# Fusing three stages of a transformer block: mixer output, row norm and the FFN up product in one program block

## The chip, the cores and the metric

The kernel runs on one core of a Trainium2 chip. The metric is device time in microseconds, the median of several runs; smaller is better. All arithmetic is float32. The large products are made of three passes in a rounded form of float32 (float32r): each factor is split into a high part (a copy rounded to float32r) and a low part (what is left), and high times high, high times low and low times high are summed.

## The reference, cut to what matters

```python
def rwkv_output(y, r, k, v, g_lo, lp):            # y: sum of a forward and a backward scan
    mu = mean(y, head); var = mean((y - mu)**2, head)
    yn = (y - mu) * rsqrt(var + GN_EPS) * ln_g + ln_b
    bonus = sum(r * k * r_k, head) * v
    return (yn + bonus) * (sigmoid(g_lo) @ g_up)

out_x = concat([y_conv, y_rwkv], -1) @ w_out      # both halves 512 wide, w_out 1024 x 1024
x = x + g1 * out_x
hx = rms_norm(x, norm2_g) * (1 + sc2) + sh2
gate, val = split(hx @ ffn_w_up, 2)               # 2816 wide each
gate = dwconv_grid(gate, 3 x 3) + b               # on a 16 x 64 grid of tokens
x = x + g2 * ((silu(gate) * val) @ ffn_w_down)
```

There are 1024 tokens and 1024 features. A second block (attention and others) follows and is not touched.

## The kernel before, in words

Activations lie feature-major: 128 partitions are 128 features, the free axis holds 1024 tokens, and KD = 8 feature tiles make the width. A PSUM bank holds 512 float32 per partition, so the tokens are worked in two halves, g = 0 and 1. Each stage is a program block of its own. Every engine has its own list of instructions, written out by hand; engines wait on semaphores. At the end of a stage all engines meet in a barrier, then the next stage starts. DMAs of these stages are issued by SyncE (SP) alone, in program order.

**scan** has 20 steps (4 over a context, 16 over the tokens, 64 tokens each), and each step does both directions (x = 0 forward, x = 1 backward). In one step TensorE's order is `token_major(s+1)`, `chain_g(s)`, `triangles`, `chain_z(s)`, `triangles`, `chain_s(s)`, `level_y`, `chain_y(s)`, `last_u`. VectorE does `triangles` (L1373), `chain_s` (L1378, L1380) and then a part of `blocks` (an inverse of small matrices, L1396 and others; its last part is in step 13). ScalarE copies TensorE's results out of PSUM, among them `chain_y`, which copies the step's output to a small buffer `yo`. SP stores it to DRAM (`store_y`, L1071, `ys`). GpSimd only makes a transposed copy five times (L1481). The results of the short convolution (`mixd`, tiles 0 to 3) and the bonus (`mixd`, tiles 4 to 7) were stored to DRAM by an earlier stage.

**mixer_out** loads forward and backward `ys` (L1511), adds them on GpSimd (L1648), and for each of four feature tiles j (PAIRS = 4) makes the group norm: head mean by a product with a matrix of ones (L1533), `centred` (L1672), square (L1600), head variance (L1544), Sqrt (L1607), reciprocal (L1678) and product (L1680), gain (L1612), bonus (L1686), gate product (L1551) and gating (L1690), high part (L1617) and low part (L1653, L1706). Then the output product: 8 output tiles n, each 2 token halves, 8 feature tiles k and 3 passes, 384 matmuls (tile 0 at L1577, the others at L105), each result added to x1 by VectorE (L1716). Weights are split as they come (L1594, L1642).

**norm_x1** works in four groups of 256 tokens: squares (L1741), sums by a product with ones (L1774), Sqrt (L1747), reciprocal (L1781), product (L1787), shift (L1760), high (L1764) and low (L1800, L1812). SP loads the first FFN weights beside it (L1806).

**ffn_up** runs a loop over 22 tiles. Each has a gate tile (s = 0) and a value tile (s = 1), each in two token halves of 24 matmuls (L105), 96 in all. ScalarE copies the gate to a grid (L1881), VectorE does nine taps (L1930, L1928), ScalarE takes Silu (L1887), VectorE multiplies with the value (L1936). The next tile's weights are split by ScalarE (L1875) and GpSimd (L1904); the high part of s = 1 is split only after the Silu.

## Time and profile before

| what | value |
|---|---|
| time, median of 3 runs | 2567.75 us (2562.33 to 2571.12) |
| the profiled execution's own time | 2575.16 us |
| its span, first to last instruction | 2573.4 us |
| busy: TensorE, VectorE, ScalarE, GpSimd | 2255.2, 1483.8, 847.4, 567.9 us |
| mean granted TensorE clock | 0.942 |

The stages follow one another in time, so the time of a stretch between two barriers can be read off the timeline. The busy shares over the whole span are averages over stages with different limits. A matmul's listed duration is longer than its share of TensorE's time, because matmuls overlap: the rate is read from starts.

### The profile page before, as it was taken

To read this page: it belongs to the slowest core of one execution; us is meant where nothing else is said; L and a number is where in the kernel's file an instruction comes from. 1 tells how busy PE (TensorE), PEld (TensorE's weight loads), DVE (VectorE), ACT (ScalarE), POOL (GpSimd) and SP (SyncE) were. 2 spreads that over 40 slices of the span, in tenths; PEclk is the share of its full clock that TensorE was granted. 3 is DMA by queue.
4 is the path that set the end of the run, shared out by engine and by line. 5 is a ranking of instruction groups with operands and counts; after the bars stand their busy time and mean duration, and the time that the engine had idled before them with its cause. 6 is when DMAs were issued, how large, how long until landed. Compare 5 with 4: busy or idle time off the path is not lost. (4 is left out here: it accounts for less than half of the span.)

```text
span 2573.4 us, 44358 instructions
## 1 busy us (share of the span) xinstructions
PE 2255.2 (88%) x18308; PEld 1777.2 (69%) x18308; DVE 1483.8 (58%) x1859; ACT 847.4 (33%) x1291; POOL 567.9 (22%) x256
## 2 busy tenths in 40 slices
PE   6879999558989779599999996889999999999898
PEld 1747777458988557478887885767767766676566
DVE  5886776777663352566666664026364656735653
ACT  4333444123323321433333322125243433423321
POOL 0334443100000141322222221323422111111111
PEclk8989999879999889799999998999999999999899
DMA  6644234666565510021221114342321111011412
GB/s 255 227 149 135 101 111 145 179 165 158 131 152 130 229 42 33 17 73 73 73 73 63 64 69 151 118 141 79 126 83 55 52 58 58 34 50 42 180 66 74
DMA packets 261015, 271.14 MB, mean 105 GB/s; under 512 B 173544, under 2 KB 204904, under 8 KB 255600
## 3 DMA queue, kind: packets, MB, share of 16 engines
q1 hardware_dynamic: 256240, 251.94, 30.6%
q10 hardware_dynamic: 4608, 16.78, 1.8%
q8 instruction: 128, 2.10, 0.4%
q14 instruction: 39, 0.32, 0.0%
HBM read 200.48 MB, written 68.19 MB: 104 GB/s over the span
## 5 line engine op out<-in xcount | busy, mean ns | idle before, releaser
L105 PE MATMUL b_ps<-h_hi,b_wpool 128*128 128x512 f32 (+1 forms) x976 | 301.9, 387 | 19.6 <-issue 7.5
L105 PE MATMUL e_ps<-h_hi,e_w_hi 128*128 128x512 f32 x704 | 276.0, 392 | 32.6 <-POOL e_w_lo L1904 32.2
L1928 DVE SCALAR_TENSOR_TENSOR e_acc<-e_grid,vec,e_acc 128x1024 f32<-128x1024 f32 x176 | 265.6, 1509 | 42.7 <-DVE e_acc L1928 37.4
L105 PE MATMUL e_ps<-h_lo,e_w_hi 128*128 128x512 f32 x704 | 274.8, 390 | 0.0
L105 PE MATMUL e_ps<-h_hi,e_w_lo 128*128 128x512 f32 x704 | 274.6, 390 | 0.0
L2451 PE MATMUL g_ps<-g_h_hi,w 128*128 128x512 f32 x784 | 260.0, 403 | 4.9 <-ACT g_q L2644 4.9
L105 PEld LDWEIGHTS b_ps<-h_hi,b_wpool 128*128 128x128 f32 x976 | 183.4, 193 | 68.3 <-issue 20.3
L1904 POOL TENSOR_TENSOR e_w_lo<-raw_up,e_w_hi 128x1024 fp32r<-128x1024 f32 x44 | 115.4, 2624 | 372.6 <-ACT e_w_hi L1875 372.6
L2764 POOL TENSOR_TENSOR w<-raw_down,w 128x1024 fp32r<-128x1024 f32 x38 | 93.8, 2469 | 462.9 <-ACT w L2622 462.9
L105 PE MATMUL b_ps<-h_lo,b_wpool 128*128 128x512 f32 (+1 forms) x488 | 185.3, 380 | 0.0
L105 PEld LDWEIGHTS e_ps<-h_hi,e_w_hi 128*128 128x128 f32 x704 | 132.6, 188 | 66.4 <-issue 39.2
L2005 PE MATMUL g_pb<-g_z_hi,g_down_hi 128*128 128x512 f32 x330 | 137.3, 416 | 46.5 <-POOL g_down_lo L2147 27.3
L2451 PEld LDWEIGHTS g_ps<-g_h_hi,w 128*128 128x128 f32 x784 | 148.3, 189 | 40.5 <-ACT g_q L2644 5.6
L2451 PE MATMUL g_ps<-g_h_lo,w 128*128 128x512 f32 x392 | 155.5, 397 | 0.0
L105 PEld LDWEIGHTS e_ps<-h_hi,e_w_lo 128*128 128x128 f32 x704 | 132.6, 188 | 27.7
L105 PEld LDWEIGHTS e_ps<-h_lo,e_w_hi 128*128 128x128 f32 x704 | 132.6, 188 | 27.0
L2147 POOL TENSOR_TENSOR g_down_lo<-raw_down,g_down_hi 128x1408 fp32r<-128x1408 f32 x29 | 93.9, 3242 | 198.0 <-ACT g_down_hi L2063 198.0
L2005 PE MATMUL g_pb<-g_z_hi,g_down_lo 128*128 128x512 f32 x330 | 135.0, 409 | 0.0
L2005 PE MATMUL g_pb<-g_z_lo,g_down_hi 128*128 128x512 f32 x330 | 134.2, 407 | 0.0
L2005 PEld LDWEIGHTS g_pb<-g_z_hi,g_down_hi 128*128 128x128 f32 x330 | 65.0, 197 | 65.3 <-POOL g_down_lo L2147 29.4
L105 PEld LDWEIGHTS b_ps<-h_lo,b_wpool 128*128 128x128 f32 x488 | 94.4, 194 | 17.2 <-issue 1.8
L714 POOL TENSOR_TENSOR b_wpool<-raw_in,b_wpool 128x1024 fp32r<-128x1024 f32 x26 | 66.9, 2573 | 170.4 <-ACT b_wpool L512 170.4
(345 smaller groups left out, 4658.1 us busy)
## 6 DMA issues: line engine op xcount, KB each, us to landing
raw_up<-w_ffn SPq DMA_DIRECT2D x22, 1024.0 KB, 5.0
raw_down<-w_down SPq DMA_DIRECT2D x32, 704.0 KB, 4.1
c_op<-ops SPq DMA_DIRECT2D x40, 512.0 KB, 4.5
raw_down<-w SPq DMA_DIRECT2D x38, 512.0 KB, 3.8
b_xin<-ada_rows ACTq DMA_DIRECT2D x32, 512.0 KB, 5.3
ops<-b_xin SPq DMA_DIRECT2D x16, 1024.0 KB, 4.0
raw_in<-w SPq DMA_DIRECT2D x26, 512.0 KB, 4.3
zs<-e_z SPq DMA_DIRECT2D x22, 512.0 KB
```

Source lines behind the costliest of these rows:

```text
L105: last = nc.tensor.matmul(out, w[:, k, :], x[:, k, cols], start=(k == 0 and n == 0), stop=(k == nk - 1 and n == 2))
L714: TT(weights(s)[1], raw, weights(s)[0].bitcast(F32), ALU.subtract).then_inc(sem("lo"), 1)
L1904: nc.gpsimd.tensor_tensor(w_lo[:, s], raw[:, s], w_hi[:, s].bitcast(F32), ALU.subtract).then_inc(sem(f"lo{s}"), 1)
L1928: a = nc.vector.scalar_tensor_tensor(out=acc[:], in0=view, scalar=wt, in1=acc[:], op0=ALU.mult, op1=ALU.add)
L2005: mm = nc.tensor.matmul(ps[j % 2], w[s][:, k], y[:, f], start=(f == 0 and i == 0), stop=(f == NFF - 1 and i == 2))
L2147: nc.gpsimd.tensor_tensor(w_lo[w_slot(n)], raw[:, n % 2], w_hi[w_slot(n)].bitcast(F32), ALU.subtract).then_inc(sem(f"w_lo{n % 2}"), 1)
L2451: mm = nc.tensor.matmul(out_bank, ww[w % 2][:, k], xx[g][:, k], start=(k == 0 and a == 0), stop=(k == KD - 1 and a == 2))
L2764: nc.gpsimd.tensor_tensor(w_lo[w % 2], raw[:, w % 2], w_hi[w % 2].bitcast(F32), ALU.subtract).then_inc(sem("lo"), 1)
```

## The change

The three stages become one block, `mix_up`, and the end of `scan` prepares it.

In `scan`: the outputs stay in SBUF in a buffer `y` over all tokens. The first direction to reach a token tile (steps 4 to 11) is copied there by ScalarE; in steps 12 to 19 (`MET` = 12) VectorE adds the other direction to it out of PSUM. The stores of `ys` and the wait for them are gone. SP loads the four convolution tiles in step 10, two half tiles of `w_out` in step 11 and three in step 17, and GpSimd splits the convolution tiles and the first three weight tiles into high and low parts after its last transposed copy.

In `mix_up`: each output tile is made in two parts. The convolution part (k = 0 to 3) starts at once and is interleaved by hand with the group norm; it is added to x1 from two PSUM banks. The scan part (k = 4 to 7) follows, token half 0 for all tiles and then token half 1. Squares of the new x1 are summed on VectorE (`fold`), and one product with ones per half gives the row sums. While TensorE does the scan part of half 1, the norm of half 0 is made, and the first FFN tile starts with half 0 of both s, then half 1. Roots are made by Ln and Exp on ScalarE in place of Sqrt and VectorE's reciprocal. The loop over the other 21 FFN tiles is as before.

```diff
 # scan
+        hc = sb("hc", [P, KD // 2, 2, SEQ], F32R)
+        y = sb("y", [P, PAIRS, SEQ])
+        w1_raw = sb("w1_raw", [P, 2, KD // 2, P])
+        w1_hi, w1_lo = sb("w1_hi", [P, 3, KD // 2, P], F32R), sb("w1_lo", [P, 3, KD // 2, P], F32R)
-                for x in DIRS if s and has_y(s - 1) else ():
-                    store_y(x, s - 1)
+                if s == 10:
+                    load_conv()
+                if s == 11:
+                    for n in range(2):
+                        load_w1(n)
+                if s == 17:
+                    for n in range(2, 5):
+                        load_w1(n)
 # scan, ScalarE: chain_y
-                wait(f"stored{s % 2}_", x, 16 * ((s - NCTX) // 2))
-                copy(yo[x][s % 2][:], half(bank[x][2], 1)).then_inc(S("yo", x), 1)
+                copy(y[:, :, tokens(x, s)], half(bank[x][2], 1)).then_inc(S("yo", x), 1)
-                if has_y(s):
+                if NCTX <= s < MET:
                     both_dirs(chain_y, s)
 # scan, VectorE
+            def chain_y(x, s):
+                wait("p_y", x, s + 1 - NCTX)
+                wait("yo", 1 - x, 2 * MET - 1 - s - NCTX + 1)
+                part = y[:, :, tokens(x, s)]
+                TT(part, part, half(bank[x][2], 1), ALU.add).then_inc(S("yo", x), 1)
                 for x in DIRS:
                     chain_s(x, s)
+                for x in DIRS if s >= MET else ():
+                    chain_y(x, s)
                 T, part = (s + 6) // BATCH, (s + 6) % BATCH
                 if T < NBATCH:
                     blocks(T, part)
 # scan, GpSimd, after the last transposed copy
+            for k in range(KD // 2):
+                pool.wait_ge(sem(f"hc{k}"), 16)
+                nc.gpsimd.tensor_copy(hc[:, k, 0], hc[:, k, 1].bitcast(F32)).then_inc(sem("hc_hi"), 1)
+                pool.wait_ge(sem("hc_hi"), k + 1)
+                nc.gpsimd.tensor_tensor(hc[:, k, 1], hc[:, k, 1].bitcast(F32), hc[:, k, 0].bitcast(F32), ALU.subtract).then_inc(sem("hc_lo"), 1)
+            for n in range(3):
...
 # mix_up, SP
+            load_x(0)
+            sp.dma_start(sg, d["sgs"]).then_inc(sem("gate_in"), 16)
+            sp.dma_start(g_up, d["g_up"]).then_inc(sem("gate_in"), 16)
+            load_x(1)
+            for j in range(PAIRS):
+                sp.dma_start(bonus[j], d["mixd"][:, CONV + j]).then_inc(sem(f"bonus_in{j}"), 16)
+            for n in range(2):
+                load_w2(n)
+            for n in range(2, KD):
+                load_x(n)
+            load_w2(2)
+            load_w1(5)
+            load_w2(3)
+            load_w1(6)
+            load_w2(4)
+            load_w1(7)
+            for n in range(5, KD):
+                load_w2(n)
+            sp.wait_ge(sem("mix_lo"), PAIRS)
+            sp.dma_start(raw[:], d["w_ffn"][0]).then_inc(sem("raw_first"), 16)
 # mix_up, TensorE
+            def conv_part(n, g):
+                if n >= 3:
+                    pe.wait_ge(sem("w1_lo"), n - 2)
+                if n:
+                    pe.wait_ge(sem("added"), 2 * (n - 1) + g + 1)
+                for k in range(CONV):
+                    for m, (w, a) in enumerate(((w1_hi, 0), (w1_hi, 1), (w1_lo, 0))):
+                        mm = nc.tensor.matmul(part_ps[g][:], w[:, n % 3, k], hc[:, k, a, cols(g)], ...)
+                mm.then_inc(sem("part"), 1)
+            mean(0)
+            conv_part(0, 0)
+            mean(1)
+            conv_part(0, 1)
+            var(0)
+            mean(2)
+            conv_part(1, 0)
+            var(1)
+            gating(0)
+            mean(3)
+            conv_part(1, 1)
+            var(2)
+            conv_part(2, 0)
+            gating(1)
+            conv_part(2, 1)
+            var(3)
+            conv_part(3, 0)
+            gating(2)
+            conv_part(3, 1)
+            conv_part(4, 0)
+            gating(3)
+            conv_part(4, 1)
+            for n in range(5, KD):
+                for g in G:
+                    conv_part(n, g)
+            for n in range(KD):
+                scan_part(0, n)
+            scan_part(1, 0)
+            sums(0)
+            for n in range(1, KD):
+                scan_part(1, n)
+            for s, g in [(0, 0), (1, 0), (0, 1), (1, 1)]:
+                if g == 1 and s == 0:
+                    sums(1)
...
+            with nc.tensor.Fori(1, NFF) as i:
 # mix_up, ScalarE
+            def root(j):
+                r = rstd[:, j % 2]
+                act.wait_ge(sem("p_var"), j + 1)
+                A(r, vars_[:], ACT.Ln, scale=1.0 / HEAD, bias=t["c_gneps"]).then_inc(sem("ln"), 1)
+                act.wait_ge(sem("ln"), j + 1)
+                A(r, r, ACT.Exp, scale=-0.5).then_inc(sem("root"), 1)
+            squares(0)
+            squares(1)
+            w1_high(3)
+            root(0)
+            squares(2)
+            w2_high(0)
+            w2_high(1)
+            gained(0)
+            root(1)
+            mix_high(0)
+            squares(3)
+            gained(1)
+            w1_high(4)
+            root(2)
+            w2_high(2)
+            gained(2)
+            mix_high(1)
+            w1_high(5)
+            root(3)
+            w2_high(3)
+            gained(3)
...
 # mix_up, VectorE
+            centred(0)
+            centred(1)
+            add_conv(0, 0)
+            add_conv(0, 1)
+            centred(2)
+            normed(0)
+            add_conv(1, 0)
+            with_bonus(0)
+            gated(0)
+            normed(1)
+            centred(3)
+            with_bonus(1)
+            add_conv(1, 1)
+            normed(2)
+            add_conv(2, 0)
+            with_bonus(2)
+            gated(1)
+            add_conv(2, 1)
+            normed(3)
+            add_conv(3, 0)
+            with_bonus(3)
+            gated(2)
...
+            for k in range(1, KD):
+                fold(0, k)
+                add_scan(*((0, k + 1) if k + 1 < KD else (1, 0)))
+            add_scan(1, 1)
+            pre(0, 0)
+            pre(0, 1)
+            fold(1, 1)
+            for k in range(2, KD, 2):
+                add_scan(1, 1 + k // 2)
+                pre(0, k)
+                normed_low(0, k - 2)
+                pre(0, k + 1)
+                fold(1, 1 + k // 2)
...
+            for k in range(KD):
+                pre(1, k)
+                if k >= 2 and k % 2 == 0:
+                    normed_low(1, k - 2)
```

`pre` is the product of x1, gain and root. For even k ScalarE makes the high part in one pass and VectorE the low part (`normed_low`); for odd k ScalarE shifts and copies in two passes and GpSimd makes the low part. `w2_high`, `w1_high` split 512 elements per partition, as do `fold`, `pre` and the half-token copies.

## Rows read from the trace of the kernel before

**Rows 1.** Windows: busy time and count by engine, clock, DMA share, GB/s
```profile
840.00:862.00 22.00, 21.51 (x692) 21.04 (x686) 6.14 (x12) 7.71 (x22) 0.00 (x0) 1.00 0.12 27
873.00:922.00 49.00, 28.31 (x47) 11.00 (x47) 39.58 (x21) 21.36 (x21) 26.23 (x8) 0.74 0.66 268
922.00:1012.00 90.00, 88.09 (x386) 72.14 (x384) 22.35 (x24) 9.73 (x9) 17.63 (x8) 1.00 0.07 24
1012.00:1066.00 54.00, 19.13 (x67) 15.23 (x66) 28.71 (x43) 31.66 (x46) 15.54 (x6) 0.69 0.06 20
1089.00:1558.00 469.00, 461.40 (x2019) 377.03 (x2017) 300.36 (x234) 141.12 (x145) 108.34 (x41) 1.00 0.20 71
```

**Rows 2.** Timeline, scan's end to the output product: start, length, engine, operation
```profile
861.65 0.38 ACT L1295 ACTIVATE c_yo<-c_ps 128x256 f32<-128x256 f32 x1 [1.04 <-PE c_ps L1171]
865.29 0.33 SPq L1511 DMA_DIRECT2D d_y<-ys  x1
...
895.78 1.88 PE L1544 MATMUL d_ps<-d_sq,con 128*128 128x512 f32 x4
...
922.26 1.07 PE L1577 MATMUL d_ps<-h_hi,d_w_hi 128*128 128x512 f32 x1
```

**Rows 3.** Groups by line in 862 to 922: busy, mean ns | idle before
```profile
L1678 DVE RECIPROCAL d_rstd<-d_rstd 128x1024 f32<-128x1024 f32 x4 | 26.2, 6546 | 1.9 <-ACT d_rstd L1607 1.9
```

**Rows 4.** Timeline, the end of the output product, the norm, the first FFN tile
```profile
1011.99 0.39 PE L105 MATMUL d_ps<-h_hi,d_w_lo 128*128 128x512 f32 x1
...
1065.85 0.76 PE L105 MATMUL e_ps<-h_hi,e_w_hi 128*128 128x512 f32 x1 [24.96 <-POOL e_w_lo L1904]
...
1089.46 0.39 PE L105 MATMUL e_ps<-h_hi,e_w_hi 128*128 128x512 f32 x1
```

**Rows 5.** Timeline of VectorE, steps 12 and 13 of the scan
```profile
757.36 3.80 DVE L1396 TENSOR_TENSOR c_mul<-c_nb,c_ui 128x2048 f32<-128x2048 f32 x1
...
766.82 1.48 DVE L1373 TENSOR_TENSOR c_lt<-c_ps,con_mixer 128x512 f32<-128x512 f32 x2
...
772.95 3.67 DVE L1396 TENSOR_TENSOR c_mul<-c_ui,c_wi 128x2048 f32<-128x2048 f32 x1
...
780.92 0.69 DVE L1373 TENSOR_TENSOR c_lt<-c_ps,con_mixer 128x512 f32<-128x512 f32 x1 [1.98 <-PE c_ps L1171]
```

**Rows 6.** Timeline of ScalarE, output copy of the second direction, steps 12 and 13
```profile
760.05 0.38 ACT L1295 ACTIVATE c_yo<-c_ps 128x256 f32<-128x256 f32 x1 [1.02 <-PE c_ps L1171]
...
775.64 0.38 ACT L1295 ACTIVATE c_yo<-c_ps 128x256 f32<-128x256 f32 x1 [1.02 <-PE c_ps L1171]
```

**Rows 7.** Timeline, a tap of the first FFN tile beside GpSimd's subtraction, and the tap after
```profile
1080.59 2.43 POOL L1904 TENSOR_TENSOR e_w_lo<-raw_up,e_w_hi 128x1024 fp32r<-128x1024 f32 x1 [12.72 <-ACT e_w_hi L1875]
1081.03 3.07 DVE L1928 SCALAR_TENSOR_TENSOR e_acc<-e_grid,vec,e_acc 128x1024 f32<-128x1024 f32 x1 [0.26 <-DVE e_acc L1930]
1084.36 1.28 DVE L1928 SCALAR_TENSOR_TENSOR e_acc<-e_grid,vec,e_acc 128x1024 f32<-128x1024 f32 x1 [0.26 <-DVE e_acc L1928]
```

**Rows 8.** Timeline of ScalarE in a later stage, a root by Ln and Exp
```profile
1767.81 1.28 ACT L2083 ACT_TABLE_LOAD   x1
1769.11 0.69 ACT L2083 ACTIVATE g_v<-g_pb,eps 128x512 f32<-128x512 f32 x1
1769.81 1.28 ACT L2088 ACT_TABLE_LOAD   x1
1771.11 0.63 ACT L2088 ACTIVATE g_v<-g_v 128x512 f32<-128x512 f32 x1
```

**Rows 9.** Groups by line in 922 to 1066, x1's addition
```profile
L1716 DVE SCALAR_TENSOR_TENSOR x<-d_ps,mod,x 128x512 f32 x16 | 11.9, 751 | 67.1 <-PE d_ps L105 65.5 <-PE d_ps L1577 1.5
```

**Rows 10.** Timeline of ScalarE and GpSimd around the first FFN tile's end
```profile
1078.86 0.60 ACT L1881 ACTIVATE e_grid<-e_ps 128x512 f32<-128x512 f32 x1 [3.56 <-PE e_ps L105]
...
1098.54 2.38 POOL L1904 TENSOR_TENSOR e_w_lo<-raw_up,e_w_hi 128x1024 fp32r<-128x1024 f32 x1 [15.52 <-ACT e_w_hi L1875]
```

**Rows 11.** Waits of TensorE in 620 to 760: us in total, times, longest
```profile
PE c_ps L1197 <- DMA c_vc<-vts: 6.6, 3, 3.3
```

More of the change, by code:

```diff
@@ L1855, in _, with mean, var @@
         def _(pe):
-            with nc.tensor.Fori(0, NFF) as i:
+            def mean(j):
+                if j:
+                    pe.wait_ge(sem("centred"), j)
+                for g in G:
+                    mm = nc.tensor.matmul(means[:, cols(g)], t["c_headones"], y[:, j, cols(g)], start=True, stop=True)
+                mm.then_inc(sem("p_mean"), 1)
+            def var(j):
+                pe.wait_ge(sem("sq"), j + 1)
+                if j:
+                    pe.wait_ge(sem("ln"), j)
+                for g in G:
+                    mm = nc.tensor.matmul(vars_[:, cols(g)], t["c_headones"], sq[:, j % 2, cols(g)], start=True, stop=True)
+                mm.then_inc(sem("p_var"), 1)
@@ new lines, in gating @@
+            def gating(j):
+                if j == 0:
+                    pe.wait_ge(sem("gate_in"), 32)
+                else:
+                    pe.wait_ge(sem("gated"), j)
+                for g in G:
+                    mm = nc.tensor.matmul(gates[:, cols(g)], g_up[:, P * j:P * (j + 1)], sg[:, cols(g)], start=True, stop=True)
+                mm.then_inc(sem("p_gate"), 1)
+            def conv_part(n, g):
[5 more added lines that the diff above has]
+                    for m, (w, a) in enumerate(((w1_hi, 0), (w1_hi, 1), (w1_lo, 0))):
+                        mm = nc.tensor.matmul(part_ps[g][:], w[:, n % 3, k], hc[:, k, a, cols(g)], start=(k == 0 and m == 0),
+                                              stop=(k == CONV - 1 and m == 2))
+                mm.then_inc(sem("part"), 1)
@@ new lines, in scan_part @@
+            def scan_part(g, n):
+                q = KD * g + n
+                pe.wait_ge(sem("w2_lo"), n + 1)
+                pe.wait_ge(sem("added"), 2 * KD - 1 + q)
+                for k in range(CONV):
+                    if q == 0:
+                        pe.wait_ge(sem("mix_lo"), k + 1)
+                    for m, (w, x) in enumerate(((w2_hi, hi), (w2_hi, lo), (w2_lo, hi))):
+                        mm = nc.tensor.matmul(part_ps[q % 2][:], w[:, n, k], x[:, CONV + k, cols(g)], start=(k == 0 and m == 0),
+                                              stop=(k == CONV - 1 and m == 2))
+                mm.then_inc(sem("part"), 1)
@@ L1868, in split_hi @@
+            w1_high(6)
+            w2_high(4)
+            w1_high(7)
+            mix_high(3)
+            for n in range(5, KD):
+                w2_high(n)
             def split_hi(n, s):
                 if isinstance(n, int):
-                    act.wait_ge(t["ahead"]("up"), 16)
+                    act.wait_ge(sem("raw_first"), 16)
                 else:
@@ new lines, in _ @@
+            w1_low(3)
+            w2_low(0)
+            w2_low(1)
+            mix_low(0)
+            w1_low(4)
+            w2_low(2)
+            mix_low(1)
+            w1_low(5)
+            w2_low(3)
+            mix_low(2)
+            w1_low(6)
+            w2_low(4)
+            w1_low(7)
+            mix_low(3)
+            for n in range(5, KD):
+                w2_low(n)
+            pool.wait_ge(sem("part"), 2 * KD)
+            split_lo(1)
+            for g in G:
+                for k in range(1, KD, 2):
+                    normed_low(g, k)
@@ L1909, in _ @@
+            with_bonus(3)
+            gated(2)
+            add_conv(3, 1)
+            add_conv(4, 0)
+            gated(3)
+            add_conv(4, 1)
+            dve.wait_ge(sem("gated"), PAIRS)
             for b in range(4):
```

538 lines of the change are left out of this document (215 added, 323 removed).

## Prediction

> **What bounds the kernel now.** I read the windows first, stage by stage [rows 1]. The end of the scan keeps TensorE busy 21.5 of 22 us, the output product 88 of 90, and the FFN loop 461 of 469 at full clock: 21 tiles in 469 us are 22.3 us each, and 96 matmuls at the rate below are 21.8. These are bounds by TensorE and the change leaves their matmuls alone. Between them lie two stretches with other limits: 873 to 922, where TensorE is busy 28 of 49 us, and 1012 to 1066, with 19 of 54. Then the timeline gives the borders. The scan's last copy ends at 862.0, the first load of the next stage is issued at 865.3, and the first product matmul starts at 922.3 [rows 2]. The product's last matmul starts at 1012.0, the first FFN matmul at 1065.9, the second FFN tile at 1089.5 [rows 4]. From 862.0 to 1089.5 are 227.5 us, and this is what the change can shorten. In the first gap the reciprocals alone hold VectorE 26.2 us [rows 3].
>
> **Prices.** 384 product matmuls lie between the starts 922.3 and 1012.0, with 2 us of idle and 0.7 of slow start inside: 87 us or 0.227 us each [rows 2, 4]. A head product of 1024 tokens is four records in 1.88 us, 1.8 from start to start [rows 2]. An addition to x1 is 0.75 us [rows 9]. I take other passes over 512 elements at 0.65 to 0.7 on VectorE and 0.6 to 0.7 on ScalarE, over 1024 at 1.1 to 1.3, as their like in [rows 7, 8, 10], and GpSimd's subtraction at 2.4 for 1024 and half of it for 512 [rows 10].
>
> **The scan.** Removed: 32 small stores and their place in SP's queue. TensorE waited for scan loads only 6.6 us in all of 620 to 760 [rows 11], so this gives 0 to 4 us; I take 2. Added: (1) VectorE's `chain_y` stands ahead of `blocks` in steps 12 and 13. `blocks` starts at 757.4, but the output it would now wait for is read only at 760.05 [rows 5, 6]; with 0.4 for the addition the start moves to 760.5, 3.1 us later. The triangles at 766.8 follow `blocks` without a wait, and TensorE waits for them, so 3.1 stand on the path. In step 13 the start moves from 773.0 to 776.1, but VectorE had 1.98 us to spare at 780.9 [rows 5, 6]: 1.1. From step 14 on no `blocks` follows. (2) SP's four convolution loads of 512 KB are put ahead of step 13's operands. 2.1 MB at 268 GB/s [rows 1] are 7.8 us; about one step of 15 us covers them. I take 1.5, bounds 0 to 6. (3) Seven copies and seven subtractions on GpSimd come after 781. They keep VectorE off for their length: a tap begun beside a subtraction took 3.07 us, the next 1.28 [rows 7]. In the last steps VectorE is busy 6 of 22 us [rows 1] and only its one multiplication per direction and step reads two SBUF tensors. I take 0.4, bounds 0 to 8. Sum of the scan: +4 us, bounds -4 to +14. The last w1 loads in step 17 wait for GpSimd, but no scan load is behind them in SP's queue.
>
> **The entry.** From the last copy to the first load are 3.3 us, with the landing of a store inside that goes. I take 1.3 for what is left: the new block starts at 863.3 on the old clock of events. The head products need no load, sum or first weights, all of which the old stage waited for.
>
> **Convolution part with the group norm.** TensorE: 192 x 0.227 = 43.6, and twelve head and gate products x 1.8 = 21.6, so 65 us. The rest is beside it if nothing stalls: VectorE has 4 x 5 us of norm and 16 x 0.75, ScalarE about 30 us with the roots, GpSimd about 25. But lists are in order. I walked through them. At about +15 us ScalarE reaches `w2_high(0)`, whose load stands behind 3.9 MB (x, gate, bonus): 15 us at 268 GB/s, so it costs little; `w2_high(2)` stands behind 7.9 MB, 29 us, and is reached at +30. Behind each root hang `normed`, then an addition on VectorE, then the matmuls of the next tile but one. A root costs Ln 1.2, table load 1.28, Exp 1.1, with one more load ahead of it that shows when ScalarE has no idle time [rows 8]. TensorE then stalls about 2 us at tile 2, 2 at tile 3 and up to 6 at tile 4, where `gating(3)` waits for `gated(2)`; the start is late by these, less what the idle of others gives back. I take 5.5 for it and 1.5 for GpSimd holding VectorE's passes. Sum 72 us, bounds 65 to 87 (above: four norms one after another at 16 us each and 19 us of matmuls behind the last). `mix_low(3)` ends about 6 us after `gating(3)`, and 19 us of matmuls cover it.
>
> On the tables the row shows one load of 1.28 us between Ln and Exp and the next pass 0.02 us behind the load [rows 8]. The Trainium skill, "ScalarE: Activation LUTs", section "Table sets: the hidden batching unit", says that Ln followed by Exp needs one load, since one set has both, at about 2.7 us with its drain. The trace of this kernel does not agree in either point. If the set were shared, the loads after the first would go, which is the third case below.
>
> **Scan part and first FFN tile.** Half 0: 96 x 0.227 = 21.8 us; VectorE needs 1.4 per tile, TensorE 2.7, no stall. Half 1: 21.8 and 0.9 for the sums; VectorE has addition, two products, a low part and a fold per tile in the middle, 3.5 us against 2.7, and two banks of slack: +3.1, so 25.8. Then half 0 of the FFN tile, 48 x 0.227 = 10.9, whose inputs are ready. It covers the last fold. Then sums, Ln, table load and Exp of half 1 on the path: 0.9 + 0.2 + 0.7 + 1.3 + 0.6 = 3.7. VectorE's eight products and the low parts pace the matmuls: last input at about 11.2 after the root, then 0.7 and the value tile's 5.4. TensorE idles some 5 us and runs in pieces for 10 more. In 1012 to 1066, in like pieces, it was granted 0.69 on average [rows 1], between the two levels 1.2 and 2.4 GHz; 2 us for that. Together 34.0, bounds 28 to 40. The norm stage's 54 us become 3 + 3.7 + 11 + 2 of exposed time, and it needs no own barrier.
>
> The first tile ends at 863.3 + 72 + 21.8 + 25.8 + 34.0 = 1016.9, against 1089.5: -72.6.
>
> **The loop.** The gate's second half now ends 5.4 us before the tile's end, where it was 10.9. The low part of the next tile's value weights was there at 1098.5 + 2.4 = 1100.9, 22.3 us after the gate's end at about 1078.6 [rows 10]. Now TensorE is there 16.3 us after it and waits 6, where it waited 0.7: +5.3, once. In the second tile both halves stand as before, so the loss is not repeated.
>
> **Sum.** -72.6 + 5.3 + 4 = -63.3 us. The profiled execution's own time is 2575.2, 7.4 over the median 2567.75, so it would become 2512 and the median 2504.5. I forecast 2505.
>
> **Rivals.** (a) The forecast, 2488 to 2520. (b) The norm chain sets the pace of the convolution part: the loads arrive later than at 268 GB/s, or GpSimd's 25 us hold VectorE's two-SBUF passes each time. For it: a pass of 1.28 took 3.07 once [rows 7]. Against: 43.6 us of matmuls are independent of the chain. It costs 15 more: 2520. (c) TensorE alone sets the pace: no stall in the convolution part (-7), none in half 1 (-3), a shared table set or faster hand-over, and the scan gains: 2487. (d) The scan lengthens by 14, from loads, VectorE's waits and GpSimd: 2515 to 2528. For it: the scan is bound at every step by a loop over three engines. Against: busy shares of VectorE and GpSimd are low there [rows 1]. (e) The other side: the phase of the first tile does not heal, and each of 21 tiles waits 5.3 us again for the value weights: 21 x 5.3 = 111 against 68.6 saved: 2610. It decides from 3.3 us a tile on. Against: after tile 1 the order inside the loop is the old one, which kept TensorE busy 461 of 469 us [rows 1]. (f) Nothing moves within 0.3%: would need stalls of 60 us; that the gaps are real is in [rows 1].
>
> **How the numbers follow.** (a) 0.62, (b) 0.12, (c) 0.13, (d) 0.08, (e) 0.03, (f) 0.02. The range takes (a) to (d) without their far tails: 2482 to 2528. Faster by over 0.3% (about what a measurement of this kernel can tell from no change): 0.95; within 0.3%: 0.02; slower: 0.03.
>
> **What would show it.** Right: TensorE over 85% busy between the scan's end and the loop, clock 1.0 in most of it; no reciprocal; first product matmul within 4 us of the scan's last; the second FFN tile near 1017 + 4; one wait of about 6 us for the value weights there. Scan steps 12 and 13 longer by 3 and 1 us. Wrong: gaps of over 6 us before `gating` or part 4, table loads absent, steps 14 to 17 longer by more than 1 us each, or FFN tiles at over 22.5 us.

## The result and the profile after

The changed kernel takes 2502.15 us (median of 4 runs, 2498.41 to 2507.99) against 2569.43 (4 runs, 2562.33 to 2571.91): a ratio of 0.974, 95% interval 0.972 to 0.977. In a second series it was 2512.06 against 2568.73, ratio 0.978 (0.974 to 0.981). The forecast was 2505, range 2482 to 2528. The profiled execution took 2507.99 us, its span is 2506.2, the mean granted clock 0.951.

I cut both spans at the same five marks. They are starts of TensorE's rows in the timeline: the scan's first and last matmul (tile `c_ps`), the first matmul of the second FFN tile, and the last of the FFN loop.

| stretch | before, us | after, us | change | my term |
|---|---|---|---|---|
| up to the scan's first matmul | 493.9 | 494.1 | +0.2 | 0 |
| scan, first to last matmul | 367.4 | 360.5 | -6.8 | +4 |
| from there to the second FFN tile | 228.2 | 156.0 | -72.2 | -72.6 |
| from there to the loop's last matmul | 468.2 | 477.4 | +9.2 | +5.3 |
| from there to the end | 1015.7 | 1018.2 | +2.5 | 0 |

The windows of the kernel after, of the stages that answer to [rows 1] (us; then busy time and count of TensorE, its weight loads, VectorE, ScalarE, GpSimd; granted clock, DMA share, GB/s):

```profile
832.00:855.40 23.40, 22.89 (x743) 22.27 (x737) 8.20 (x17) 6.85 (x20) 0.00 (x0) 1.00 0.02 4
856.80:928.50 71.70, 67.28 (x242) 46.45 (x243) 30.95 (x32) 39.05 (x41) 27.58 (x17) 0.98 0.44 154
928.50:950.50 22.00, 22.00 (x96) 17.66 (x95) 12.04 (x16) 6.33 (x9) 4.81 (x2) 1.00 0.13 48
950.50:974.00 23.50, 21.06 (x87) 15.74 (x85) 18.10 (x23) 14.93 (x22) 4.73 (x3) 1.00 0.00 1
974.00:1010.00 36.00, 29.18 (x108) 21.86 (x109) 19.40 (x21) 17.66 (x24) 9.98 (x6) 0.86 0.00 1
1010.60:1055.30 44.70, 38.31 (x158) 31.16 (x157) 25.95 (x23) 13.33 (x14) 7.41 (x3) 0.92 0.20 71
1055.30:1491.00 435.70, 424.82 (x1861) 347.86 (x1859) 280.82 (x217) 127.67 (x132) 100.91 (x38) 1.00 0.19 69
```

The two stretches in which TensorE was busy 28 of 49 and 19 of 54 us are gone. In their place are a convolution part that keeps TensorE busy 67 of 72 us, a first half of the scan part that is full, and an end part that is busy 29 of 36. In the sixth row stands the price in the loop: 38 of 45 us busy and a clock of 0.92, in the tiles that follow the first.

TensorE's rows at the borders, and its long waits (start, length, instruction, in brackets the idle time before it and what ended it):

```profile
856.86 1.96 PE L1610 MATMUL e_means<-c_y,con 128*128 128x512 f32 x4 [1.86 <-PEq L83]
...
891.51 0.70 PE L1637 MATMUL e_part<-c_hc,c_w_hi 128*128 128x512 f32 x2 [0.68 <-DVE x L1924]
...
902.84 0.70 PE L1637 MATMUL e_part<-c_hc,c_w_hi 128*128 128x512 f32 x2 [3.69 <-DVE x L1924]
...
994.90 1.19 PE L1701 MATMUL e_vars<-h,e_w_hi 128*128 128x512 f32 x2 [5.58 <-DVE h L1953]
...
1028.05 1.19 PE L105 MATMUL e_gates<-h,e_w_hi 128*128 128x512 f32 x2 [6.39 <-POOL e_w_lo L1873]
```

The new block begins at 856.9, 1.4 us after the scan's last addition to `c_y` ends at 855.5. The first matmul of the scan part starts at 928.1, the first FFN matmul at 977.4, and the second FFN tile at 1010.6. The part between 856.9 and 928.1 has two waits, 4.4 us together. The last two rows are the wait for the row norm's second half and the wait for the value weights of the second tile. Both matmuls behind them take 1.19 us a pair, where the like of them take 0.62 at full clock.

### The profile page after: what moved, and what is told of

It reads as the page before. It is cut to its first block and busy times, and to the rows that moved or that the text cites. A ratio compares the mean times of both kernels' runs of the same rounds, so it can differ in the third digit from the quotient of the medians.

```text
span 2506.2 us, 44088 instructions
## 1 busy us (share of the span) xinstructions
PE 2241.5 (89%) x18248; PEld 1768.3 (71%) x18248; DVE 1478.6 (59%) x1876; ACT 853.1 (34%) x1290; POOL 568.2 (23%) x275
## 5 line engine op out<-in xcount | busy, mean ns | idle before, releaser
L105 PE MATMUL e_gates<-h,e_w_hi 128*128 128x512 f32 x672 | 210.0, 394 | 14.7 <-POOL e_w_lo L1873 14.5
L105 PE MATMUL e_vars<-h,e_w_hi 128*128 128x512 f32 x672 | 206.9, 389 | 0.0
L1873 POOL TENSOR_TENSOR e_w_lo<-e_raw_up,e_w_hi 128x1024 fp32r<-128x1024 f32 x44 | 115.6, 2627 | 377.4 <-ACT e_w_hi L1809 377.4
L105 PEld LDWEIGHTS e_gates<-h,e_w_hi 128*128 128x128 f32 x672 | 126.4, 190 | 45.6 <-issue 19.4
L105 PEld LDWEIGHTS e_vars<-h,e_w_hi 128*128 128x128 f32 x672 | 126.1, 188 | 26.2
L105 PE MATMUL e_gates<-h,e_w_lo 128*128 128x512 f32 x336 | 131.9, 392 | 0.0
L105 PE MATMUL e_vars<-h,e_w_lo 128*128 128x512 f32 x336 | 130.7, 389 | 0.0
```

Source lines behind the costliest of these rows:

```text
L105: last = nc.tensor.matmul(out, w[:, k, :], x[:, k, cols], start=(k == 0 and n == 0), stop=(k == nk - 1 and n == 2))
L1873: TT(w_lo[:, s], raw[:, s], w_hi[:, s].bitcast(F32), ALU.subtract).then_inc(sem(f"lo{s}"), 1)
```

## Experiments

**Does the scan's gain belong to the change?** The pair of traces shows a scan that is 6.8 us shorter, where I had put +4. Before I explain such a number I want to know its scatter, so both kernels were profiled again, unchanged.

> The kernel before, unchanged, profiled once more. The question is how much the scan's end moves from one execution to another. Theory (the scan's gain of 6.6 us is the change's own): the second direction's last scan copy of this stage again starts at 858.8, within 2 us. Rival (it is chance in how loads meet): it comes out anywhere between 850 and 866.

> The changed kernel, unchanged, profiled once more and timed. Theory: the last scan copy again at 852.2 within 2 us, first product mean at 856.9, and the time 2502 +- 4 us. Rival (chance): the scan's end differs by 5 us or more between two executions of the same kernel, and then the 6.6 us of the pair of traces say nothing.

Measured: the scan's last matmul that reads `c_sc` starts at 861.2 in the first trace of before and at 852.6 in the second; of the changed kernel at 854.5 and 861.1. The order of the pair has turned round. The rival (chance) is right. To see where the scatter is, I measured the time from one step's product `c_sc<-c_s,pend` of the second direction to the next step's, 19 intervals in each trace. An interval is read like this, from VectorE's timeline of the changed kernel; it is the 13th and lasts from 752.26 to 768.75, 16.49 us:

```profile
752.26 0.43 DVE L1396 TENSOR_TENSOR c_sc<-c_s,pend 128x256 f32<-128x256 f32 x1
753.89 0.42 DVE L1377 TENSOR_TENSOR c_y<-c_y,c_ps 128x256 f32<-128x256 f32 x1 [1.20 <-PE c_ps L1182]
755.29 0.42 DVE L1377 TENSOR_TENSOR c_y<-c_y,c_ps 128x256 f32<-128x256 f32 x1 [0.98 <-PE c_ps L1182]
755.63 3.82 DVE L1412 TENSOR_TENSOR c_mul<-c_nb,c_ui 128x2048 f32<-128x2048 f32 x1
...
766.32 1.28 DVE L1389 TENSOR_TENSOR c_mt<-c_ps,con_mixer 128x512 f32<-128x512 f32 x2
767.51 0.41 DVE L1394 TENSOR_TENSOR c_s<-c_sc,c_ps 128x256 f32<-128x256 f32 x1
...
768.75 0.42 DVE L1396 TENSOR_TENSOR c_sc<-c_s,pend 128x256 f32<-128x256 f32 x1
```

Sums over these intervals, all traces (the kernels in the lower rows are told of below; "scan as changed" are the ones whose scan is that of the changed kernel):

| trace | 1 to 10 | 11, 12 | 13 | 14 to 19 | all |
|---|---|---|---|---|---|
| before | 172.3 | 31.0 | 15.59 | 86.7 | 305.6 |
| before_again | 167.5 | 29.0 | 15.60 | 86.2 | 298.3 |
| before_y_ahead | 171.4 | 32.3 | 16.46 | 84.5 | 304.7 |
| scan as changed, mean of 6 | 165.8 | 35.7 | 16.50 | 84.1 | 302.1 |
| lowest and highest of the 6 | 161.8, 169.4 | 32.7, 39.0 | 16.46, 16.53 | 83.0, 85.2 | 296.2, 305.5 |
| waits_back | 166.7 | 37.1 | 16.46 | 82.5 | 302.7 |
| y_behind_blocks | 162.7 | 32.7 | 21.34 | 86.9 | 303.6 |
| conv_loads_late | 163.9 | 30.7 | 16.53 | 88.2 | 299.3 |
| best | 166.0 | 31.8 | 16.47 | 86.8 | 301.0 |

Intervals 1 to 12 move by some 8 us from one execution to another. Interval 13 agrees within 0.07 us and the sum of 14 to 19 within 2.2, and there a single trace can be believed for differences above that. Over all, the scan of the changed kernel is as long as before, 302.1 against 301.9 in the two traces of before, with some 4 us of doubt. The last stretch of the table at the top, 1000 us that no edit touches, scatters too: 1007.6 to 1021.9 in 14 traces. That is why I judge the experiments below by their stage in the trace, and name times of whole kernels only beside before's median of the same series.

**The removed stores.** First only their waits:

```diff
+            def store_y(x, s):
+                wait("yo", x, s + 1 - NCTX)
 ...
+                for x in DIRS if s and has_y(s - 1) else ():
+                    store_y(x, s - 1)
                 if s == 10:
                     load_conv()
```

> Only SP's waits for the scan output are back in its list, without the stores: the queue stands still as long as before but no bytes move. The output is the same. If the queue's order is what held the scan (a load behind a wait): the last scan copy at 860, the kernel 8 us slower than the changed one. If it is the 14,400 small packets of the stores that delay the loads: no difference to the changed kernel (852, 2502).

Measured: 2511.94 us against 2568.73, where the unchanged changed kernel had 2512.06 in the same series; intervals 1 to 10 are 166.7, within the others' scatter. SP's waits alone cost nothing that shows. The stores themselves in their old number and from the buffer `y` were not measured: VectorE's addition could write there what a store still reads. They were put back from a constant tensor, in a dose that stands out of the scatter:

```diff
+                for copy in range(4):
+                    sp.dma_start(d["ys"][copy, x, :, :, at:at + C].rearrange("q p c -> p q c"),
+                                 t["con"][:, 0:PAIRS * C].rearrange("p (q c) -> p q c", q=PAIRS)).then_inc(S("stored", x), 16)
```

> The changed kernel with each of the 32 stores of the scan output put back four times (128 stores of 128 KB in pieces of 256 bytes, from a constant tensor into one that nobody reads; each still waits for the scan's output in SP's list). In nine traces the steps 1 to 10 of the scan took 170 us in the kernel before and 166 in those without the stores, with 2.5 us of scatter, so one trace can't tell what the stores cost. Theory T1 (they cost 4 us): the scan is 12 to 20 us longer than 362. Rival T2 (my 2 us): 6 to 10 longer. Rival T3 (nothing; the queue and the DMA have room): within 4 us.

Measured: 2542.51 us against 2561.93. From the scan's first matmul to the new block's first are 400.0 us, where six traces of the unchanged scan have 359.3 to 368.9, mean 365.3. The 128 stores cost 35 us, 0.27 each, of which 5 are the wait for the last of them ahead of the block. That is more than either theory named. The waits of TensorE in this kernel, from 620 us to the block's start (us in total, times, longest), and then the same line of the changed kernel's second trace:

```profile
PE c_ps L1221 <- DMA c_vc<-vts: 31.7, 10, 10.6
PE e_means L1623 <- PEq L83: 6.8, 1, 6.8
```

```profile
PE c_ps L1208 <- DMA c_vc<-vts: 3.1, 1, 3.1
```

The median from issue to landing of such a load is 5.2 us with the 128 stores and 5.3 without, so the loads come late because they are issued late; the stores ahead of them in SP's list hold them up. SP's row for the eight stores of one step shows how long:

```profile
700.84 4.79 SPq L1136 DMA_DIRECT2D ys<-con  x8
```

All 128 hold SP for 79.7 us. For the real dose, 32 stores, the traces bear only the difference in intervals 1 to 10: 170.4 in the three traces that have them, 165.8 in the six without, so about 4.6 us, with a standard error of 2. The dose run is 12.5 us longer there than the six, 8.0 in 11 and 12, nothing in 13 and 9.3 in 14 to 19. A quarter of that would be 7.5, but one trace with 32 stores has 84.5 in 14 to 19 where the six have 84.1, so the cost is not in proportion to the number. I had 2.

**VectorE's `chain_y` and `blocks`.** The changed kernel with the old order on VectorE:

```diff
-                for x in DIRS if s >= MET else ():
-                    chain_y(x, s)
                 T, part = (s + 6) // BATCH, (s + 6) % BATCH
                 if T < NBATCH:
                     blocks(T, part)
+                for x in DIRS if s >= MET else ():
+                    chain_y(x, s)
```

> VectorE's addition of the scan output stands behind the block sums again in steps 12 and 13 (the old order); all else is the changed kernel. By my sum before the result this order costs 3.1 us in step 12 and 1.1 in step 13: 4 us faster, 2498. By the trace of the changed kernel, where steps 12 and 13 are 1.9 and 0.9 us longer, at most 2.8 us, and if the four convolution loads are the cause of these two instead, 0: 2502.

Measured: 2515.38 us against 2564.08. Interval 13 is not 3 us shorter but 4.8 longer, and 14 to 19 are 2.8 longer. The old order was harmless only because ScalarE did this copy then. TensorE's waits show it; its `chain_g` of the next step stands still until the output has left the bank:

```profile
754.65 0.48 PE L1182 MATMUL c_ps<-c_vc,c_mt 64*64 64x64 f32 x4 [4.82 <-DVE c_y L1377]
...
772.75 0.33 PE L1182 MATMUL c_ps<-c_vc,c_mt 64*64 64x64 f32 x4 [1.58 <-DVE c_y L1377]
```

In the changed kernel, between 745 and 800 us, TensorE waits for no `c_y` at all. So this run doesn't measure what the order alone costs; the other way round does, the kernel before with only the copy moved to VectorE and ahead of `blocks`:

```diff
-                if has_y(s):
+                if has_y(s) and s < 12:
                     both_dirs(chain_y, s)
 ...
                 for x in DIRS:
                     chain_s(x, s)
+                for x in DIRS if s >= 12 else ():
+                    wait("p_y", x, s + 1 - NCTX)
+                    ...
+                    nc.vector.tensor_copy(yo[x][s % 2][:], half(bank[x][2], 1)).then_inc(S("yo", x), 1)
```

> The kernel before, with one part of the change: from step 12 on the scan output is copied by VectorE, ahead of the block sums, and not by ScalarE. The four convolution loads aren't there. By my sum step 12 gets 3.1 us longer and step 13 1.1. In seven traces of kernels with the change's order steps 11 and 12 together took 34.1 to 39.0 us against 29.0 and 31.0 before, and 30.7 where the convolution loads came later; step 13 took 16.5 against 15.6. Theory A (the order costs 3.1): 33 to 34 for steps 11 and 12. Theory B (the loads cost it): 29 to 31, and step 13 at 16.5.

Measured: 2566.68 us in one run against 2561.93, inside the scatter. Interval 13 is 16.46, the same as in every changed kernel with this order and 0.9 above before; interval 14, which holds the last part of `blocks`, is 14.65 against 14.86 and 16.22; 14 to 19 together are 2.0 shorter, though the stores are there. Intervals 11 and 12 are 32.3, but they decide nothing between the two theories. Interval 13 starts at the product of step 12, and the moved copy comes behind that product, so it can't reach the intervals before; 32.3 is a third value beside the 31.0 and 29.0 of before. VectorE's rows of interval 13 in this kernel:

```profile
758.11 0.42 DVE L1380 TENSOR_TENSOR c_sc<-c_s,pend 128x256 f32<-128x256 f32 x1
...
761.48 3.79 DVE L1396 TENSOR_TENSOR c_mul<-c_nb,c_ui 128x2048 f32<-128x2048 f32 x1
...
772.13 1.28 DVE L1373 TENSOR_TENSOR c_mt<-c_ps,con_mixer 128x512 f32<-128x512 f32 x2
...
774.57 0.42 DVE L1380 TENSOR_TENSOR c_sc<-c_s,pend 128x256 f32<-128x256 f32 x1
```

And the end of the same interval in the kernel before, behind the triangles of [rows 5]:

```profile
769.41 0.69 DVE L1373 TENSOR_TENSOR c_mt<-c_ps,con_mixer 128x512 f32<-128x512 f32 x1 [1.11 <-PE c_ps L1171]
770.29 0.69 DVE L1373 TENSOR_TENSOR c_mt<-c_ps,con_mixer 128x512 f32<-128x512 f32 x1 [0.18 <-PE c_ps L1171]
771.22 0.42 DVE L1378 TENSOR_TENSOR c_s<-c_sc,c_ps 128x256 f32<-128x256 f32 x1 [0.24 <-PE c_ps L1171]
...
772.61 0.42 DVE L1380 TENSOR_TENSOR c_sc<-c_s,pend 128x256 f32<-128x256 f32 x1
```

`blocks` starts 3.37 us behind the product before it, where it was 0.34: 3.0 later, as I said. But behind the triangles VectorE had waits for TensorE, 1.11, 0.18 and 0.24 in the rows above, and they are gone; with shorter passes beside them 2.1 of the 3.0 come back.

**The convolution loads.**

```diff
-                if s == 10:
-                    load_conv()
+                if s in (13, 15):
+                    load_conv((s - 13) // 2)
```

> The four loads of the convolution branch of 512 KB each, ahead of step 10's operands in SP's list, go two by two into steps 13 and 15. If they lengthened steps 11 and 12 (by 1.2 and 1.9 us in the traces), the scan ends up to 3 us sooner, 2499, provided that the splits behind them on GpSimd, now 12 to 20 us later, stay hidden. If the loads are covered by the steps before them: 0. If the splits now meet VectorE's products in the last steps: 1 to 4 us slower.

Measured: 2507.67 us against 2564.08. Intervals 11 and 12 fall to 30.7, the level of before, and interval 16 is 19.6 where the six have 15.7 to 16.4. So four loads of 512 KB ahead of a step's operands cost about 4.9 us (35.7 against 30.8, the mean of the three kernels without them; traces with them from 32.7 to 39.0), and two of them cost about 3.5 in a later step.

**The tables.** In both roots a function of the same table, so that the output is another:

```diff
-                A(r, vars_[:], ACT.Ln, scale=1.0 / HEAD, bias=t["c_gneps"]).then_inc(sem("ln"), 1)
+                A(r, vars_[:], ACT.Exp, scale=-1.0 / HEAD, bias=t["c_gneps"]).then_inc(sem("ln"), 1)
```

> The logarithm in both roots (of the group norm and of the row norm) is an Exp of the same shape, so that the table never changes; the roots' values and with them the output are others. It measures what the table loads cost. By my prediction's third case (one table set for both: no stall in the convolution part, -7 us) the part takes 65 to 67 us and the end part 1.3 less: 7 us faster in all here. By the trace of the changed kernel (4.4 us of stall in the part, of which one of 3.7 at the last gate products): 3 to 5 us faster. If the loads are covered by other waits: only the 1.3 us of the last root.

Measured: 2495.59 us against 2564.08. The convolution part takes 66.3 us where it took 71.2, the scan part 48.5 where 49.4, the end part 32.1 where 33.2: 6.8 us, as much as the expectation had for a shared table. The third case of the prediction, 18 us in all, had other gains beside it, which this run doesn't show. The convolution part's window and two of ScalarE's rows:

```profile
860.50:926.80 66.30, 66.29 (x240) 45.81 (x241) 31.48 (x31) 28.84 (x33) 27.97 (x17) 0.97 0.47 167
```

```profile
879.34 1.11 ACT L1738 ACTIVATE e_rstd<-e_vars,gneps 128x1024 f32<-128x1024 f32 x1
880.49 1.06 ACT L1740 ACTIVATE e_rstd<-e_rstd 128x1024 f32<-128x1024 f32 x1
```

No load stands between the two passes, and TensorE has no idle time left: with the eight loads of 1.28 us of this part gone, the part is bound by TensorE's own 66 us. The 4.9 us are not the loads' own 10.2: they are the two waits of 4.4 together and the slow clock behind the longer one. Part 4's first half (12 products) takes 4.40 us in the changed kernel and 2.72 here; against that, the first head product here falls on the lower clock, 3.65 us where it was 1.96. The rule of the Trainium skill that I weighed before ("ScalarE: Activation LUTs", section "Table sets: the hidden batching unit": Ln and Exp share a set) would have brought this time; in the changed kernel it doesn't hold, there is a load for each change of function.

**The interleaving.** The four norms first, then the whole convolution half. The splits and additions that belong to the convolution half move behind the norms on their engines too, and the loads of one pair of weights change places:

```diff
-            conv_part(0, 0)
 ...
-            conv_part(4, 1)
-            for n in range(5, KD):
+            for n in range(KD):
```

> All four head groups of the group norm go first and the whole convolution half of the output product follows, instead of the two interleaved. Theory (the interleaving covers the norm chain with 43.6 us of independent matmuls, and this is the larger part of what the change brings): the chain alone takes 38 to 52 us, then come 43.6 us of matmuls, and the part grows from 71.2 to 82 to 96; the kernel is 11 to 25 us slower than the changed one. Rival: TensorE's 65 us are the bound in either order because the chain is short: within 3 us. Second rival: the chain sets the pace even when interleaved, then the part would be the chain's length plus little, and taking the matmuls out of it adds all 43.6: over 30 us slower. The scan is that of the changed kernel: one more sample of its steps.

Measured: 2527.76 us against 2561.93, a ratio of 0.986 (0.983 to 0.990). The part takes 95.3 us, 24.1 more. Its two halves, and what TensorE waited for in it:

```profile
859.10:908.90 49.80, 27.75 (x49) 10.46 (x49) 18.67 (x15) 33.16 (x31) 12.55 (x7) 0.83 0.44 164
908.90:954.40 45.50, 45.50 (x194) 37.16 (x193) 12.48 (x16) 6.42 (x10) 14.57 (x11) 0.96 0.20 64
```

```profile
PE e_gates L1627 <- DVE c_y L1905: 10.9, 2, 7.2
PE e_vars L1618 <- ACT e_rstd L1728: 9.8, 3, 4.3
```

The chain by itself is 49.8 us, at a clock of 0.83, and the convolution's matmuls behind it take 45.5, the first of them at the low clock. Together they are 95.3, laid into each other 71.2. This is the upper part of the range in the theory, and the chain's 49.8 hold four stops of 3.7 to 7.2 us with a slow clock behind them; the second rival would have needed a chain of 71.

**The value weights of the second tile.**

```diff
-    UP_FIRST = [(0, 0), (1, 0), (0, 1), (1, 1)]
+    UP_FIRST = [(0, 0), (0, 1), (1, 0), (1, 1)]
```

> The first FFN tile of the stage runs gate half 0, gate half 1, value half 0, value half 1, as the other tiles do in their own order, instead of gate 0, value 0, gate 1, value 1. If the wait of 6.4 us for the second tile's value weights comes from the late end of the gate's second half, as I said, it goes; but the last root is then covered by 5.4 us of matmuls less, and TensorE waits those 5.4 longer at 988. Net within 1.5 us of the changed kernel. Rival: the weight chain behind the gate also needs the value tile's end, then the wait stays and the kernel is 5 us slower.

Measured: 2500.22 us against 2564.08. The cause is as I said, but the net is not zero. The wait is 1.01 instead of 6.39, the loop is 468.9 instead of 477.4, and the end part is 33.5 instead of 33.2. The window of the loop's first 45 us, and TensorE at the sums:

```profile
1017.90:1062.60 44.70, 43.69 (x193) 35.90 (x192) 28.49 (x23) 13.68 (x14) 10.99 (x4) 1.00 0.20 71
```

```profile
989.87 1.02 PE L1655 MATMUL e_means<-e_total,con 128*128 128x512 f32 x2
996.47 1.19 PE L1701 MATMUL e_vars<-h,e_w_hi 128*128 128x512 f32 x2 [5.58 <-DVE h L1953]
```

TensorE waits the same 5.58 us for the root with one product ahead of the sum as with two. My expectation was wrong in this: a product that stands ahead of the sum in TensorE's list covers nothing of the root, since it puts off the sum too. The changed kernel's own rows say as much, ScalarE first and then VectorE's last fold:

```profile
980.17 1.28 ACT L1760 ACT_TABLE_LOAD   x1
989.36 0.69 ACT L1760 ACTIVATE e_total<-e_means,eps 128x512 f32<-128x512 f32 x1 [7.91 <-PE e_means L1655]
990.06 1.28 ACT L1762 ACT_TABLE_LOAD   x1
991.36 0.63 ACT L1762 ACTIVATE e_total<-e_total 128x512 f32<-128x512 f32 x1
```

```profile
980.18 0.69 DVE L1941 TENSOR_TENSOR e_total<-e_total,e_squared 128x512 f32<-128x512 f32 x1 [0.70 <-ACT e_squared L1756]
```

The fold is done at 980.9, the sum starts at 988.3, and ScalarE is idle 7.9 us for it. So the sum was moved up, with the products in the changed kernel's order:

```diff
-                if g == 1 and s == 0:
-                    sums(1)
 ...
                 for k in range(KD):
+                    if (s, g, k) == (0, 0, 5):
+                        sums(1)
```

> The row norm's second sum stands in TensorE's list behind the sixth of the eight inner steps of the first FFN product instead of behind both products of token half 0. In the changed kernel's trace the last fold is done 3.5 us after the first FFN matmul, but the sum starts 10.9 us after it. Theory: the root starts 7 us sooner and is covered by the rest of these products; from the first FFN matmul to the second tile 33.2 becomes 26 to 27, the wait of 6.4 us for the value weights stays: 6 to 7 us faster than the changed kernel. Rival: VectorE's pace (8 products and low parts of half 1) or a cold clock takes it back: 30 or more.

Measured: 2491.03 us against 2561.93, a ratio of 0.974 (0.970 to 0.977). From the first FFN matmul to the second tile are 25.9 us instead of 33.2, and the wait for the value weights is again 6.39. The stretch's window, TensorE at the sum, and ScalarE's first pass behind it:

```profile
971.80:997.80 26.00, 24.11 (x100) 18.04 (x99) 16.71 (x18) 16.59 (x22) 8.38 (x5) 1.00 0.00 1
```

```profile
975.35 1.12 PE L1655 MATMUL e_means<-e_total,con 128*128 128x512 f32 x2
```

```profile
976.51 0.69 ACT L1760 ACTIVATE e_total<-e_means,eps 128x512 f32<-128x512 f32 x1 [0.64 <-PE e_means L1655]
```

TensorE is busy 24 of 26 us, at a clock of 1.00 where it was 0.86. The last run joins this with the loads spread over four steps:

```diff
-                if s == 10:
-                    load_conv()
+                if 13 <= s <= 16:
+                    load_conv(s - 13)
```

> The early sum of the run before, and the four convolution loads one by one in the steps 13, 14, 15 and 16 of SP's list instead of all four in step 10. In eight traces with the four loads in step 10 the scan's steps 11 and 12 took 35.5 us on average, against 30.8 in three traces without them and 30.7 with the loads two by two in steps 13 and 15, where step 16 was 3.4 us longer. Theory: one load of 512 KB (2 us at 268 GB/s) per step is covered: steps 11 and 12 at 31, steps 14 to 19 at 84, scan 4 us shorter, about 2487 us. Rival: the loads cost about a microsecond each wherever they stand: steps 14 to 19 at 88, no gain over 2491. The stretch from the first FFN matmul to the second tile again 25.9 us.

Measured: 2496.11 us against 2566.98, a ratio of 0.973 (0.970 to 0.975). Both versions are 70.9 us under before's median of their series; the changed kernel is 56.7 and 67.3 under it. Intervals 11 and 12 are 31.8, and 14 to 19 are 86.8 where the six have 84.1. The rival is right: the loads cost much the same in either place.

## Why the prediction was right, and where it wasn't

**The first tile.** This is where the time came from. From the block's first matmul to the second FFN tile I had 153.6 us (72, 21.8, 25.8, 34.0) and the trace has 153.8 (71.2, 22.4, 27.0, 33.2). The entry is 1.4 for 1.3. The convolution part rests on two numbers, TensorE's 65 and a stall of 5.5, and both hold: TensorE alone is 66.3 in the run without table loads, of which 1.7 are a slow start, and the stalls are 4.4. I had 2 us at tile 2, 2 at tile 3 and up to 6 at tile 4; the first two have 0.7 between them and tile 4 has 3.7. The 1.5 us that I put down to GpSimd holding VectorE's passes are the slow clock behind that stall, 1.7: a term of the right size for the wrong reason. The part takes 71.1 to 72.9 us in eight traces with this order and 74.0 in the one with the 128 stores. In the four longest its first product is on the lower clock, 2.9 to 3.8 us in place of 1.96. That TensorE's other matmuls cover the norm chain is shown by the norms put first: 24 us more.

That run also splits the 72 us. From the scan's last matmul to the first product behind the norm chain were 61.0 us in the kernel before, and are 51.8 with the norms first: 9. From there to the second FFN tile were 167.2 and are 128.0: 39, for the row norm laid into the products and the barriers gone. The interleaving adds 24. Only the 24 were undone by a run; the 9 and the 39 are read from two traces, and what Ln and Exp in place of the reciprocals are worth by themselves stays open.

**Half 1 of the scan part.** 27.0 for 25.8. I gave VectorE three microseconds for its passes; TensorE's waits for `x` there are 0.5, 1.3 and 1.3, and cost 3.7 when counted from start to start. One pass of `normed_low` took 1.78 us beside GpSimd's subtraction, which I had counted in the convolution part and not here. The rest is the rate: three products of the scan part take 0.70 us from start to start, where 0.227 each makes 0.68. That is 0.6 us in either half, and half 0 is 22.4 for 21.8.

**The end part.** 33.2 for 34.0. The path to the root is 14.6 us as I had it. VectorE's and GpSimd's passes end 12.3 after it in place of 11.2, and the 2 us for a slow clock are not on the path: the clock is low from 992.6 to 1002.8, but the last input comes only at 1004.3, and the products that need it start at 1004.4. The two errors together are the 0.8. And I took the sum's place as given; it cost 7 us that the early sum got back.

**The loop.** The mechanism was right, the wait is 6.39 for 6.0 and comes once; from the third tile on they last 21.8 and 22.8 us in turn. The term was mis-sized, 9.2 for 5.3. The second tile takes 31.0 us (22.7 in the kernel before), where it takes 23.0 with the gate first: 5.4 of stall and 2.6 of matmuls that start at the lower of the two clock levels (1.19 us a pair in place of 0.62) behind it. I had charged the slow clock in the end part and forgot it here.

**The scan.** The sum of its terms, +4, was within what can be told from the +0.2 of the means, and no term that could be measured was right. The one for GpSimd's splits (0.4) no run isolates. The order of `chain_y`: 0.9 in place of 3.1, and nothing in place of 1.1. The step that failed is "The triangles at 766.8 follow `blocks` without a wait, and TensorE waits for them, so 3.1 stand on the path": I looked for slack ahead of the triangles and not behind them, where 1.5 us of waits stood. The convolution loads: about 4.9 in place of 1.5, at the upper end of my bounds; I took one step of 15 us to cover 7.8 us of transfer, but the step's operands are behind them in SP's list. The removed stores: about -4.6 in place of -2, argued from three traces against six and from the dose of 128. And a term that I had not: intervals 14 to 19 are 2.4 us shorter, which the kernel before shows too (2.0, one trace) once VectorE and not ScalarE empties the bank; why, no run shows. How loads meet stores in steps 1 to 12 stays open; one trace there is worth +-4 us.

**The number.** That 2505 came within 3 us of 2502.15 is in part luck. In the pair of traces the scan was 6.8 us shorter where I had +4, and the repeated traces show that as chance; it more than made up for the 3.9 us that the loop cost beyond what I had. In the second series the gain is 56.7 us and not 67.3. What the prediction had right is the 72 us of the first tile, and the two traces of the changed kernel agree there within 1 us.

**The rivals.** The norm chain didn't set the pace, though with 49.8 us alone beside TensorE's 65 it is near, and it causes both stalls of the part. The shared table set of the third case is what the run without table loads measures, 6.8 us, and it isn't the changed kernel. The first tile's phase heals.

## What to carry to other kernels

Work of another product, laid by hand into a chain that runs over three engines, was worth 24 us here for 44 us of matmuls; its gain could be forecast from a walk down the lists here: the total of the stalls came out, their places only in part. Where a sum or another first link of a chain stands in an in-order list behind independent work, ask when its input is ready: moved up, the same work covers the chain, and here that was 7 us. Before a difference of a few microseconds in a load-bound stage is explained, profile the same kernel twice; and each of the stops of TensorE of 3.7, 5.6 and 6.4 us here cost its length and then the slow matmuls behind it.

## What was not expected of the hardware

The scan of one and the same program differs by 7 to 9 us between executions (298.3 and 305.6 us over the 19 intervals of the kernel before, 296.2 to 305.5 of the changed one), nearly all of it in the steps in which DMA is busy two thirds of the time (its share is 0.63 to 0.66 from 540 to 740 us, in four traces). In these traces the stops of 5.6 and 6.4 us were followed each time by the lower level of the granted clock, with TensorE at half its speed: 2.6 us in the second tile. The wait of 3.7 us before part 4 of the convolution did it too, in all nine traces that have it. Only the moment differs. In the second trace the first pair of matmuls behind the wait is slow already; in the first trace the pair takes 0.70 us (shown above) and one a little later takes 1.05. The second trace, then the first:

```profile
909.39 1.19 PE L1637 MATMUL e_part<-c_hc,c_w_hi 128*128 128x512 f32 x2 [3.69 <-DVE x L1924]
```

```profile
904.68 1.05 PE L1637 MATMUL e_part<-c_hc,c_w_hi 128*128 128x512 f32 x2
```

The 12 products take 4.1 to 4.4 us in eight of the traces and 5.3 in the second of the changed kernel, where the run without table loads, which has no wait there, has 2.7.

GpSimd's subtraction also holds VectorE's passes of 512 elements. In the changed kernel, GpSimd's row and then VectorE's, one pass that meets it and one that doesn't:

```profile
970.34 1.58 POOL L1868 TENSOR_TENSOR h<-e_whole,h 128x512 fp32r<-128x512 f32 x1 [2.71 <-ACT h L1771]
```

```profile
970.69 1.78 DVE L1953 SCALAR_TENSOR_TENSOR h<-e_whole,mod,h 128x512 fp32r<-128x512 f32 x1
...
974.33 0.73 DVE L1953 SCALAR_TENSOR_TENSOR h<-e_whole,mod,h 128x512 fp32r<-128x512 f32 x1
```

By the Trainium skill ("SBUF — State Buffer", section "Who interferes with whom") a VectorE instruction with two inputs in SBUF contends with a GpSimd instruction that reads SBUF, for a shared pair of ports that is locked exclusively. The rows agree in the main: the pass began 0.35 us into the subtraction and ended 0.55 after it, so of its own 0.73 all but some 0.2 stood behind the subtraction.
